# Residual tiles loaded one column tile before their use, and the pooled branch's weights split behind the fold

## What is computed

```python
# first block, per layer
h = rmsnorm(x, norm_g); proj = h @ w_in            # three branches: differential attention,
...                                                # gated mixing, dilated attention
merged = sum(sigmoid(gate_n) * (y_n @ w_branch_n))
x = x + merged @ w_out                             # output stage: residual added

# second block, per layer
u = rms_norm(h, norm_w) @ w_in
y_f = fourier_mix(f_in)    # real part of a 2-d DFT over rows and features, times fourier_w
y_p = pool_mix(p_in)       # windowed means minus the input, times pool_w (64x64 per group), scaled
y_a = mla_mix(...)         # latent attention, 4 heads
h = h + concat(y_f*silu(f_gate), y_p*silu(p_gate), y_a*silu(a_gate)) @ w_out   # output stage
```

## Time and profile before

| | us |
|---|---|
| median of 3 runs | 3862.49 (3857.2 to 3864.9) |
| the profiled execution, its own time | 3852.36 |
| its span in the trace | 3850.6 |
| TensorE busy | 3666.1 (95%) |
| VectorE / ScalarE / GpSimd busy | 1700.0 (44%) / 1259.4 (33%) / 1086.0 (28%) |
| mean granted TensorE clock | 0.985 |

### The profile page before, as it was taken

The page is one execution under the profiler, slowest core; times in us unless marked ns, Lnnn a source line. Parts: engine busy times, 40 slices in busy tenths (PEclk is TensorE's granted clock), DMA queues, the critical chain, the costliest instruction groups (busy, mean ns, idle before and its releaser), DMA issues.

```text
span 3850.6 us, 50301 instructions
## 1 busy us (share of the span) xinstructions
PE 3666.1 (95%) x20446; PEld 3235.1 (84%) x20446; DVE 1700.0 (44%) x3146; ACT 1259.4 (33%) x2869; POOL 1086.0 (28%) x794
## 2 busy tenths in 40 slices
PE   6999998999999999999999999998999998999998
PEld 5887887878887788878778888878999998999998
DVE  5434555333345453255534333545343436424433
ACT  3112444033342121144413334323245532224541
POOL 2633222321112354323223211223530113531012
PEclk9999999999999999999999999998999999999999
DMA  3122111411014321211031111332110022111012
GB/s 111 44 69 71 33 36 53 151 36 44 32 40 146 106 69 51 85 32 44 31 129 63 42 44 39 126 128 70 47 57 15 24 67 90 65 45 38 16 43 99
DMA packets 85190, 243.81 MB, mean 63 GB/s; under 512 B 10720, under 2 KB 24800, under 8 KB 84960
## 3 DMA queue, kind: packets, MB, share of 16 engines
q1 hardware_dynamic: 84960, 240.61, 18.4%
HBM read 190.04 MB, written 50.53 MB: 62 GB/s over the span
## 4 chain that ended last, share of the span: by engine, by line
PE 72%; DVE 12%; ACT 7%; issue 4%; DMA 2%; POOL 1%; SPq 0%; DVEq 0%; POOLq 0%; ACTq 0%
PE pj L1446 28%; PE pS L1446 23%; PE po L1677 4%; PE po L1569 3%; PE pS L1657 3%; PE pS L1659 2%; DVE KK L2334 1%; DVE tmp L2322 1%; PE pS L1540 1%; DVE tmp L2325 1%; PE pS L1541 1%; ACT PT L1885 1%; PE pt L1556 1%; DMA xr<-xres 1%; DVE tmp L2319 1%
## 5 line engine op out<-in xcount | busy, mean ns | idle before, releaser
L2763 POOL TENSOR_SCALAR Whi<-stage 128x1024 fp32r<-128x1024 f32 (+3 forms) x252 | 261.3, 1037 | 1970.6 <-DMA stage<-wstream 1287.3
L1446 PE MATMUL pj<-Hhi,Whi 128*128 128x512 f32 x1640 | 659.9, 402 | 9.7 <-DVE Hlo L2187 3.6
L1446 PE MATMUL pj<-Hhi,Wlo 128*128 128x512 f32 x1640 | 643.1, 392 | 0.0
L1446 PE MATMUL pj<-Hlo,Whi 128*128 128x512 f32 x1640 | 641.5, 391 | 0.0
L2765 POOL TENSOR_TENSOR Wlo<-stage,Whi 128x1024 fp32r<-128x1024 f32 (+3 forms) x252 | 595.8, 2364 | 21.0
L1446 PEld LDWEIGHTS pj<-Hhi,Whi 128*128 128x128 f32 x1640 | 310.6, 189 | 79.7 <-ACT PT L1885 6.6
L1446 PEld LDWEIGHTS pj<-Hhi,Wlo 128*128 128x128 f32 x1640 | 309.4, 189 | 66.8
L1446 PEld LDWEIGHTS pj<-Hlo,Whi 128*128 128x128 f32 x1640 | 310.5, 189 | 59.1
L1446 PE MATMUL pS<-Hhi,Whi 128*128 128x512 f32 x792 | 314.4, 397 | 18.4 <-DVE Hlo L2187 10.6
L1446 PE MATMUL pS<-Hlo,Whi 128*128 128x512 f32 x792 | 312.0, 394 | 0.0
L1446 PE MATMUL pS<-Hhi,Wlo 128*128 128x512 f32 x792 | 312.0, 394 | 0.0
(11 more groups left out here) (462 smaller groups left out, 7671.3 us busy)
## 6 DMA issues: line engine op xcount, KB each, us to landing
stage<-wstream SPq DMA_DIRECT2D x228, 512.0 KB, 4.2
merged<-Mb SPq DMA_DIRECT2D x32, 512.0 KB, 2.9
Mb<-merged SPq DMA_DIRECT2D x32, 512.0 KB, 4.3
gates<-tmp SPq DMA_DIRECT2D x48, 256.0 KB, 2.2
TH<-gates SPq DMA_DIRECT2D x24, 512.0 KB, 5.9
xres<-X SPq DMA_DIRECT2D x16, 520.0 KB, 2.9
xr<-xres SPq DMA_DIRECT2D x16, 520.0 KB, 4.2
X<-xT SPq DMA_DIRECT2D x16, 256.0 KB, 7.4
```

The costliest lines, as they stand in the source:

```text
L1446: x = pe.e.matmul(ps, w[a][:, v.koff + k * P:v.koff + k * P + P], moving(v.of, b, k, v.t0, v.n), start=k == 0 and i == 0, stop=k == v.K - ...
L2763: pool.e.tensor_scalar(upper, stage, 1.0, 0.0, ALU.mult, ALU.add).then_inc(*pool.tick("whi", c))
```

## The change

The unit that loads the residual tile of e+1 now stands directly behind unit (e, 0), so one column tile (and on SP's queue one store and one weight load) earlier than before; tile 0 is still loaded ahead of everything. Its ring condition is the same: the last addition of row block e-1, which used this buffer. In layer 1 of block two VectorE's scaling has become a unit of its own (`residual2_scale`) and stays where it was, before (e, 0). Second, `small_in` keeps only the zeroes on VectorE (and GpSimd's zero borders), and a new unit `pw_in` behind `fold` holds ScalarE's `pwhi` and VectorE's `pwlo`.

```diff
@@ -895,20 +895,26 @@
         if last:
             self.put("tables2_in")
         r, box, inside, done = {}, {}, {}, {}
+
+        def residual_in(e):
+            r[e] = self.put("residual_in", l=l, e=e, ring=e % 2, ring_free=ring_free[e % 2],
+                            stored=self.resready[e] if self.resready else None)
         for e, i in [(e, i) for e in range(6) for i in range(2)] + [(6, 0), (7, 0), (6, 1), (7, 1)]:
             t0, n = TC1[i]
             if (e, i) == (1, 0) and last:
                 meta = self.put("meta_squares")
             if i == 0:
                 box[e] = {}
-                r[e] = self.put("residual_in", l=l, e=e, ring=e % 2, ring_free=ring_free[e % 2],
-                                stored=self.resready[e] if self.resready else None)
+            if (e, i) == (0, 0):
+                residual_in(0)
             if (e, i) == (7, 1):
                 head = self.norm_head(l + 1, sums, done)
                 inside[e, i] = {4: [head.row]}
             u = self.add(Unit(kind="proj", make="residual", key=("out1", l, e), box=box[e], of="H", K=8, koff=0, i=i, t0=t0, n=n,
                               opens=i == 0, ends=i == 1, ready=self.h_ready[i], banked=True, emptied="residual",
                               e=e, xo=xo, res_in=("res_in", r[e].id), inside=inside.get((e, i))))
+            if i == 0 and e < 7:
+                residual_in(e + 1)
             self.square("1", e, i, t0, n, ("residual", u.id), xo)
             if last:
                 self.square("g", e, i, t0, n, ("residual", u.id), xo)
@@ -1046,6 +1052,7 @@
         u = self.put("gmix", l=l, po_free=self.po_free)
         g_ready = self.po_free = ("lo", u.id)
         fold = self.put("fold", l=l, f_ready=f_ready).id
+        self.put("pw_in", l=l)
         self.run(p[1])
         dc += [self.weight(x) for x in dw[2:]]
         for j, c in enumerate(dc):
@@ -1357,12 +1364,17 @@
             scaled = ("rs", u.id)
         ytok = [self.y2tok[c] + self.ya2 for c in range(3)]
         r, box, inside, head = {}, {}, {}, None
+
+        def residual_in(e):
+            r[e] = self.put("residual2_in", l=l, e=e, ring=e % 2, ring_free=ring_free[e % 2], stored=self.resready[e])
         for e, i in [(e, i) for e in range(6) for i in range(3)] + LAST2:
             t0, n = TC2[i]
             if i == 0:
                 box[e] = {}
-                r[e] = self.put("residual2_in", l=l, e=e, ring=e % 2, ring_free=ring_free[e % 2],
-                                stored=self.resready[e], scaled=scaled)
+                if e == 0:
+                    residual_in(0)
+                if scaled:
+                    self.put("residual2_scale", e=e, ring=e % 2, of=r[e].id, scaled=scaled)
             if (e, i) in ((6, 2), (7, 2)):
 
                 rs += self.spread(sums[e - 6], within=True)
@@ -2008,7 +2022,7 @@
             act.wait_ge(u.f_ready[i])
             hi(m.fe[0][:, 0, i, 0:HALF + 1:HALF], m.Fx[i][:, 0:HALF + 1:HALF], u.id, 3 * i + 2)
 
-    def small_in(u):
+    def pw_in(u):
         act.wait_ge(("small_in", u.l))
         phase_met(u)
         for i in range(2):
@@ -2103,7 +2117,7 @@
     parts = {"phase": phase, "proj": proj, "square": square, "spread": spread, "row_spread": row_spread, "meta_squares": meta_squares,
              "norm": norm, "table": table, "mix_in": mix_in,
              "lnlow": lnlow, "yb": yb, "v_turn": v_turn, "soft": soft, "turns": turns, "values": values, "finish": finish,
-             "fold": fold, "small_in": small_in, "gmix": gmix, "amix": amix, "pool0": pool_z,
+             "fold": fold, "pw_in": pw_in, "gmix": gmix, "amix": amix, "pool0": pool_z,
              "pool1": pool_z, "unfold": unfold, "pool_out": pool_out, "values_in": values_in, "soft2": soft2,
              "turns2": turns2, "values2_rest": values2_rest, "finish2": finish2, "rope2_out": rope2_out}
     for u in order.units:
@@ -2486,14 +2500,13 @@
 
 
 
-    def residual2_in(u):
-        if u.scaled:
-            x = m.xr2[u.ring][:, META:L2]
-            dve.wait_ge(("res2_in", u.id))
-            dve.wait_ge(u.scaled)
-            phase_met(u)
-            STT(out=x, in0=x, scalar=vec[:, 52 + u.e:53 + u.e], in1=m.RSy[:, :], op0=ALU.mult, op1=ALU.mult).then_inc(
-                *dve.tick("res2_scaled", u.id))
+    def residual2_scale(u):
+        x = m.xr2[u.ring][:, META:L2]
+        dve.wait_ge(("res2_in", u.of))
+        dve.wait_ge(u.scaled)
+        phase_met(u)
+        STT(out=x, in0=x, scalar=vec[:, 52 + u.e:53 + u.e], in1=m.RSy[:, :], op0=ALU.mult, op1=ALU.mult).then_inc(
+            *dve.tick("res2_scaled", u.of))
 
 
 
@@ -2584,11 +2597,14 @@
 
 
 
-    def small_in(u):
+    def pw_in(u):
         phase_met(u)
         for i in range(2):
             dve.wait_ge(("hi", "pw", u.l, i))
             lo(m.pw[1][:, i, :], m.fc[4 + i][:, :], m.pw[0][:, i, :], "pw", u.l, i)
+
+    def small_in(u):
+        phase_met(u)
         for a, b in ((HALF, LP), (0, 1)):
             for i in range(2):
                 dve.e.memset(m.fe[i][:, :, :, a:b].bitcast(F32), 0.0).then_inc(*dve.tick("zeroes", u.l, a, i))
@@ -2735,7 +2751,7 @@
     parts = {"phase": phase, "start": start, "clear": clear, "square": square, "sums": sums, "last_sums": last_sums, "norm": norm,
              "table": table, "proj": proj,
              "mix_in": mix_in, "ln": ln, "lnlow": lnlow, "lnmix": lnmix, "yb": yb, "merge_end": merge_end, "soft": soft, "values": values,
-             "finish": finish, "residual2_in": residual2_in, "small_in": small_in, "gmix": gmix, "fold": fold, "amix": amix,
+             "finish": finish, "residual2_scale": residual2_scale, "small_in": small_in, "pw_in": pw_in, "gmix": gmix, "fold": fold, "amix": amix,
              "pool0": pool0, "pool1": pool1, "unfold": unfold, "mark3": mark3, "pool_out": pool_out, "soft2": soft2,
              "turned_last": turned_last, "values2_rest": values2_rest, "finish2": finish2, "last": last,
              "rope2_out": rope2_out}

```

## The result

| | us |
|---|---|
| kernel before, median of 6 runs | 3858.35 (3854.01 to 3864.90) |
| kernel after, median of 6 runs | 3835.96 (3827.05 to 3843.99) |
| ratio after / before, 95% interval | 0.9942 (0.9924 to 0.9959) |
| profiled execution of after, its own time | 3843.26 (span 3841.5) |

The change makes the kernel 22 us faster (16 to 29 by the interval). Forecast were 3836 us and a gain of 26.8. The profiled execution is one of the longer ones of the six, so its end is not the place to look: it was 9.8 us late before anything that changed in block two, at 2515.74 against 2505.97, mostly by half-clock stretches that come and go from one execution to the next in unchanged code.

What follows compares the result with a forecast made beforehand. TensorE, busy 95% of the span, bounds the kernel; only its waits and half-clock stretches can yield time. 6.0 + 8.2 + 2 x (1.4 + 4.9) = 26.8 us off the median 3862.5 gives 3836 us, range 3819 to 3851.

Steps and rivals of the forecast that it cites:

- Residual tile, block one: Output stage of layer 2: the 3.01 us wait before the row sums goes, plus 3.3 clock, 0.3 given back: 6.0 us.
- granted clock 1.00 behind them: Sign of being right: TensorE at full clock behind the row sums of the two output stages that gain.
- Residual tile, block two: Output stage of layer 1: the 5.86 us wait before the sums goes, plus clock behind it: 8.2 us (bounds 3 and 8.5).
- The other two stages: Output stages of block one's layer 1 and the last: no gain, since no DMA-caused wait stands before their sums.
- Pooled weights, the wait: Before `amix`, the fold ends sooner: 1.4 us per layer (bounds 0 and 2.6), TensorE's wait falls to about 1.1.
- Pooled weights, the clock: Behind the fold, full clock in place of 0.50: 7.3 us per layer, counted at two thirds, 4.9.
- The kernel before need not fall in each execution: Behind the fold: three of four waits of 2.1 to 2.6 us fell, so two thirds of the clock gain counted.
- At 1.1 us I expect it to hold: Behind the fold: after a remaining wait of 1.1 us the clock stays at 1.00.
- The rival with both folds at full gain: Both folds fell in every execution before, none after: all 31.6 us gained, 3831 us; chance 0.15.
- `pwlo` ahead of `Alo`: Behind the fold: the two subtractions moved there fit into VectorE's idle 2.69 us.
- `lv` first: Behind the fold: `pwlo` just after GpSimd's `lv` starts ends at about 2668.2, making the sum 0.3 us worse per layer.
- The slower rival: Second block's attention: the clock could fall there; 80 us at half clock would give 3876 us; chance 0.03.

Runs made afterwards that it cites:

- out2_only: Kernel before with only block two's residual tiles sent early, block one's tiles and the pooled weights as before; 0.9986 of the time before.
- pw_only: Kernel before with only the pooled weights' split moved behind the fold, all residual tiles as before; 0.9984 of the time before.
- fill_before: Kernel before plus 14 useless matmuls of 348 columns in each fold's wait for VectorE; 0.9961 of the time before.
- pw_twice: Kernel before with VectorE's two subtractions for `pwlo` done twice ahead of the fold; 1.0014 of the time before.
- warm2: fold_early plus useless fp32 matmuls where TensorE waits at more places of block two; 0.9928 of the time before.
- after_again: Kernel after, without an edit, measured once more beside the kernel before; 0.9936 of the time before.
- fold_early: Kernel after with the whole fold moved ahead of the last column tile of the first pooled projection; 0.9923 of the time before, median 3824.8 us.
- fill_sums: Kernel before plus useless matmuls in the waits before the row sums, 14 in block one and 18 in block two; 0.9989 of the time before.

## Why the prediction was right

The time came out as forecast (3836.0 against 3835.96), and the mechanisms were the ones named: early tiles end the waits before the sums, the shorter fold ends most of the wait before `amix`, and both give back clock. That the digits agree is luck. The forecast started from a median of three runs before, 3862.5 us, where six runs say 3858.35; the gain was forecast at 26.8 us and measured at 22.4 (16 to 29), and 24.7 the second time. By the lengths most terms were somewhat too large. Step by step:

- **Residual tile, block one: 6.0 forecast, 6.3 measured (S1).** The wait is gone, additions are released by TensorE. The split was 3.0 for the wait and 3.3 for the clock; measured are 3.9 up to the sums and 2.4 behind them. The wait is 3.8 to 4.3 us in the profiles of out2_only, pw_only, fill_before and pw_twice, where the one execution at hand had shown 3.0. The clock was counted as if it would read 1.00 behind the sums; it reads 0.79 there with no wait at all, which the prediction's sign "granted clock 1.00 behind them" had not allowed.
- **Residual tile, block two: 8.2 forecast, 7.2 measured (S2).** The clock's part is 2.7 us, where 2.35 were counted, and here it reads 1.00 behind the sums. The wait's part was counted too high, at the 5.86 us of the one execution at hand. This wait reads 2.9 to 6.5 us in the five profiles with late tiles, 4.5 on average, and the sums come 4.5 us sooner with the tiles early.
- **The other two stages: nothing.** From 3742.40 before (3733.09 after) to the last sums' spread the last stage took 99.6 us and 99.8. The output stage of layer 1, block one, was 90.7 us before, 92.4 after. Of the eight kernels with the edit there, after and warm2 had a half-clock stretch at its start (0.83 over 10 us, 92.4 and 92.3 us), and after_again took 90.1 us but waited 2.7 us for the weight split `Wlo` right behind it, where the kernel before waited 1.25; the other five and the six without the edit read 90.7 to 90.8. Whether the early tiles make such losses likelier, this many profiles don't tell.
- **Pooled weights, the wait: 1.4 per layer forecast, 1.5 and 1.3 measured,** 1.1 us left forecast, 0.98 and 1.21 measured. The first addition came 0.64 us behind `Ghi` (0.7 forecast), and one addition met GpSimd's `Dlo` for 2.36 us, as the step had allowed.
- **Pooled weights, the clock: 4.9 per layer forecast;** from the first `amix` product to the first cosine product it took 13.4 and 13.7 us with the fold as before and 8.9 and 10.0 with the edit, 4.5 and 3.6 less, and 0.4 and 0.3 went behind it: 3.7 on average. The term was too large, and its reasons held only by half. "The kernel before need not fall in each execution" was wrong: with waits of 2.3 us and more the clock was at 0.57 in all ten folds seen, and at 0.50 in the two of pw_twice. "At 1.1 us I expect it to hold" was wrong as well: it held through `amix` in five folds with waits of 0.84 to 1.00 us, but fell at the cosine products behind each of them, and it fell within `amix` at 0.86, 1.01 and 1.21. These two errors have opposite signs. The rival with both folds at full gain (3831) had the kernel before right and the one after wrong.
- **`pwlo` ahead of `Alo`: no cost, as forecast.** The two subtractions took 0.48 us and `Alo` waited 1.88 us for ScalarE behind them. They came 0.2 us ahead of GpSimd's `lv`, so the case that was priced at 0.3 us, `lv` first, didn't arise. In fold_early it did: there GpSimd was at work and the same two took 1.92 us. That agrees with the Trainium skill, "SBUF — State Buffer", section "SBUF: two separate sides", on the port pair held for the whole instruction.
- **The slower rival** (the second block's attention at half clock) did not happen: 0.99 over 250 us, before and after.

## What to carry to other kernels

Price a wait of the bounding engine with the clock behind it: look at the granted clock of the stretch that follows, and at what is awaited at that stretch's end. If it is another engine's work that doesn't depend on TensorE's in the stretch, the clock is worth nothing there (warm2); if it does depend on it, most of the clock arrives (fill_sums, 1.8 of 2.4 us). A short unit that needs nothing and is read late should stand behind the chain that TensorE waits for, and where a whole chain can be started one column tile sooner (fold_early) that is better than shaving it. Where a wait can't be removed, useless products into a bank that is overwritten anyway can be worth more than they cost, but only where TensorE's work behind them is what comes last afterwards; this is to be tried, not assumed.

## What the hardware showed that was not expected

- Behind waits of TensorE of 2.3 to 3.1 us ahead of `amix` the granted clock fell to the lower of its two levels every time (ten folds, 0.57 over 20 us). Behind 0.84 to 1.21 us, eight folds, it read 0.66 to 0.91, never 1.00. With no wait there or with useless products, after which 0.66 and 0.80 us of wait were left in fill_before (eight folds), it read 1.00 six times, 0.91 and 0.83 once each. Where a given execution lands is not settled by the wait's length alone: 0.84 kept the clock through `amix`, 0.86 did not.
- With no wait at all the clock still read 0.79 in the 8 us behind the row sums of block one, in all eight kernels with early tiles. TensorE had done 32 products of one column there in 2.3 us. Behind the 6 such products of block two (0.5 us) it read 1.00. What makes the difference was not tested.
- 28 useless products of 348 columns, 4.4 us of work, made the kernel 15 us faster (9.6 to 20.4).
- Over code that is the same but for its first output stage, the distance between the starts of the two output stages of block one was 1279 to 1288 us over the executions profiled; the mean granted clock over it was 0.993 in the shortest and 0.983 in the longest. That is the size of this change's parts, and lengths between fixed instructions inside one profile told them apart where medians of 5 to 11 runs could not.
